# Feed-forwards of both streams: the next chunk's first inner tile ahead of a chunk's products down

## The reference

```python
def swiglu(h, w_in, w_out):
    a, b = jnp.split(h @ w_in, 2, axis=-1)
    return (jax.nn.silu(a) * b) @ w_out      # w_in 1024 x 5632, w_out 2816 x 1024

def _mlp(h, w1, w2):
    return jnp.square(jax.nn.relu(h @ w1)) @ w2   # w1 1024 x 4096, w2 4096 x 1024
```

## Time and profile before

| | |
|---|---|
| median of 3 runs | 3189.69 us (3185.83 to 3190.51) |
| the profiled execution's own time | 3183.49 us |
| its span | 3181.7 us |
| PE busy | 2898.7 us, 91% of the span |
| DVE, ACT, POOL busy | 1940.5, 1177.5, 549.0 us |
| granted TensorE clock, mean | 0.945 of full speed |
| HBM read | 408.60 MB, 129 GB/s over the span |

### The profile page before, as it was taken

The page is one execution under the profiler, slowest core; times in us unless marked ns, Lnnn a source line. Parts: engine busy times, 40 slices in busy tenths (PEclk is TensorE's granted clock), DMA queues, the critical chain, the costliest instruction groups (busy, mean ns, idle before and its releaser), DMA issues.

```text
span 3181.7 us, 38322 instructions
## 1 busy us (share of the span) xinstructions
PE 2898.7 (91%) x15190; PEld 2369.1 (74%) x15190; DVE 1940.5 (61%) x3141; ACT 1177.5 (37%) x1953; POOL 549.0 (17%) x561
## 2 busy tenths in 40 slices
PE   3899999988899998999998799899799998988797
PEld 2788887545788887888787799764777787845797
DVE  7888855645777857878555765542456664434554
ACT  3222234343422234222355554334432223335552
POOL 0000010322100010000101110113421113035431
PEclk7999999978999999999999899999899999989898
DMA  6556522101455534555322255220144432332453
GB/s 244 192 193 209 184 75 93 47 27 40 144 194 199 204 113 165 198 202 189 104 100 67 81 189 186 97 66 15 52 149 162 149 137 74 108 75 44 130 182 107
DMA packets 125283, 412.16 MB, mean 130 GB/s; under 512 B 25088, under 2 KB 27136, under 8 KB 124464
## 3 DMA queue, kind: packets, MB, share of 16 engines
q1 hardware_dynamic: 109552, 353.07, 33.1%
q0 software_dynamic: 15552, 56.63, 5.1%
HBM read 408.60 MB, written 1.05 MB: 129 GB/s over the span
## 4 chain that ended last, share of the span: by engine, by line
PE 80%; DVE 8%; ACT 7%; issue 2%; POOL 2%; DMA 1%; POOLq 0%; SPq 0%; ACTq 0%; DVEq 0%
PE bank L2132 24%; PE bank L2134 24%; PE bank L2133 24%; PE bank L2327 2%; POOL sb_temp L1124 1%; DVE sb_split_low L1664 1%; ACT sb_split_high L1266 1%; DVE sb_temp L1678 1%; PE bank L2288 1%; PE bank L2472 1%; DVE sb_rstd L1720 1%; DVE sb_temp L1728 1%; DVE sb_h_low L1734 1%; PE bank L2471 1%; PE bank L2317 1%
## 5 line engine op out<-in xcount | busy, mean ns | idle before, releaser
L2132 PE MATMUL bank<-sb_h_high,sb_split_high 128*128 128x256 f32 (+1 forms) x3048 | 1063.5, 349 | 107.2 <-DVE sb_h_low L1734 48.0
L2133 PE MATMUL bank<-sb_h_low,sb_split_high 128*128 128x256 f32 (+1 forms) x3048 | 1041.6, 342 | 0.0
L2134 PE MATMUL bank<-sb_h_high,sb_split_low 128*128 128x256 f32 (+1 forms) x3048 | 1040.8, 341 | 0.0
L1664 DVE TENSOR_TENSOR sb_split_low<-sb_raw,sb_split_high 128x1024 fp32r<-128x1024 f32 x515 | 639.0, 1247 | 237.0 <-ACT sb_split_high L1266 233.4
L2132 PEld LDWEIGHTS bank<-sb_h_high,sb_split_high 128*128 128x128 f32 x3048 | 592.4, 194 | 195.9 <-issue 61.9
L1266 ACT ACTIVATE sb_split_high<-sb_raw 128x1024 fp32r<-128x1024 f32 x515 | 536.0, 1050 | 369.5 <-DMA sb_raw<-weights 369.3
L2133 PEld LDWEIGHTS bank<-sb_h_low,sb_split_high 128*128 128x128 f32 x3048 | 595.0, 195 | 67.1 <-issue 0.5
L2134 PEld LDWEIGHTS bank<-sb_h_high,sb_split_low 128*128 128x128 f32 x3048 | 593.4, 195 | 67.0
L1678 DVE CUSTOM_DVE_ANT_0 sb_temp<-sb_ada_ffn,sb_cond_ffn 128x1024 bf16<-128x1024 f32 x408 | 479.5, 1219 | 11.8 <-ACT sb_cond_ffn L1270 8.1
L1784 DVE SCALAR_TENSOR_TENSOR sb_x_res<-bank,sb_gates,sb_x_res 128x256 f32<-128x256 f32 x296 | 133.1, 478 | 282.2 <-PE bank L2134 281.8
L2132 PE MATMUL bank<-sb_hidden_high_ffn,sb_split_high 128*128 128x512 f32 (+1 forms) x788 | 272.7, 346 | 0.0
(11 more groups left out here) (260 smaller groups left out, 3211.6 us busy)
## 6 DMA issues: line engine op xcount, KB each, us to landing
sb_raw<-weights SPq DMA_DIRECT2D x515, 512.0 KB, 3.3
sb_ada_ffn<-ada SPq DMA_DIRECT2D x114, 512.0 KB, 4.3
sb_ada_ffn<-ada POOLq DMA_DIRECT2D x90, 512.0 KB, 3.5
sb_ada_mlp<-ada SPq DMA_DIRECT2D x18, 512.0 KB, 4.2
sb_ada_mlp<-ada POOLq DMA_DIRECT2D x18, 512.0 KB, 4.3
sb_cond_ffn<-cond SPq DMA_DIRECT2D x3, 1024.0 KB, 5.3
sb_na_raw<-na_rpb SPq DMA_DIRECT2D x32, 96.0 KB, 5.8
sb_x_res<-tokens SPq DMA_DIRECT2D x1, 2048.0 KB, 15.4
```

The lines of the kernel that those rows point to most:

```text
L1664: do.tensor_tensor(m.low[i][:, :], m.raw[i][:, :], m.high[i][:, :].bitcast(F32), ALU.subtract).then_inc(*dve.mark("split_low", s))
L2132: do.matmul(out, ah, bh, start=start and j == 0, stop=False)
L2133: do.matmul(out, ah, bl, start=False, stop=False)
L2134: last = do.matmul(out, al, bh, start=False, stop=stop and j == len(terms) - 1)
```

## The change

While a chunk's products down are due, the first inner tile of the next chunk is worked out ahead of them: its up pieces come before the down pieces. `AHEAD = 1` is the number of such tiles, `ups_at` gives the first tile whose up pieces belong to a chunk, and the weight stream is laid out in the new order. One more hidden tile is held (`n_hidden`: nine buffers instead of eight in the stages of several chunks), and tile h lies in buffer h modulo that number, so that ACT's wait is for the chunk of the tile that lay there before. Stages of one chunk stay as they are.

```diff
--- before.py
+++ after.py
@@ -147,11 +147,12 @@
 
 def chunks(up, down, sizes):
 
-    n_up, out, at = len(up) // len(down), [], 0
+    n_up, out, at, done = len(up) // len(down), [], 0, 0
     for n in sizes:
         blocks = down[at:at + n].reshape(n, P, DT, P).transpose(2, 0, 1, 3).reshape(n, 8, P, P)
-        out += [up[at * n_up:(at + n) * n_up], blocks.transpose(0, 2, 1, 3).reshape(n, P, SLAB)]
         at += n
+        out += [up[done * n_up:(at + AHEAD) * n_up], blocks.transpose(0, 2, 1, 3).reshape(n, P, SLAB)]
+        done = at + AHEAD
     return np.concatenate(out)
 
 
@@ -161,6 +162,8 @@
           ("mla_down", 7), ("mla_uq", 6), ("mla_ukv", 4), ("mla_out", 8), ("mlp0", 64),
           ("na_fm", 16), ("na_tm", 8), ("na_out", 8), ("mlp1", 64)]
 N_SLABS = sum(n for _, n in STREAM)
+
+AHEAD = 1
 
 SIZES = {"ffn00": (8, 7, 7), "ffn01": (8, 7, 7), "ffn10": (8, 7, 7), "ffn11": (22,), "mlp0": (8, 8, 8, 8), "mlp1": (32,)}
 
@@ -321,11 +324,8 @@
 
 def up_slab(f, h, ab):
 
-    s, at = SLAB0[f], 0
-    for n in SIZES[f]:
-        if h < at + n:
-            return s + (h - at) * n_up(f) + ab
-        s, at = s + n * n_up(f) + n, at + n
+    c = next(c for c in range(len(SIZES[f])) if h < ups_at(f, c + 1))
+    return SLAB0[f] + h * n_up(f) + ab + chunk_at(f, c)
 
 
 def chunk_at(f, c):
@@ -333,8 +333,18 @@
     return sum(SIZES[f][:c])
 
 
+def ups_at(f, c):
+
+    return min(chunk_at(f, c) + AHEAD, sum(SIZES[f])) if c else 0
+
+
 def down_slab(f, c, block):
-    return SLAB0[f] + chunk_at(f, c + 1) * n_up(f) + chunk_at(f, c) + block // 8
+    return SLAB0[f] + ups_at(f, c + 1) * n_up(f) + chunk_at(f, c) + block // 8
+
+
+def n_hidden(f):
+
+    return max(SIZES[f]) + (AHEAD if len(SIZES[f]) > 1 else 0)
 
 
 def last_up(f):
@@ -466,7 +476,7 @@
     first = [[piece for h in range(head // per) for piece in up_pieces(f, h, part, ring)] for part in (0, 1)]
     body = []
     for c, n in enumerate(sizes):
-        for h in range(chunk_at(f, c), chunk_at(f, c + 1)):
+        for h in range(ups_at(f, c), ups_at(f, c + 1)):
             if h >= head // per:
                 body += up_pieces(f, h, p, ring)
         last = c == len(sizes) - 1
@@ -939,7 +949,7 @@
             self.bv = self.sb("na_bv", (P, D), own=own)
 
     def feed_forward_memory(self, f, own):
-        n = max(SIZES[f])
+        n = n_hidden(f)
         width = T if FFN[f][3] == BOTH else NX_TOK
         if FFN[f][2]:
             self.ada[f] = [self.sb(f"ada{i}_{f}", (P, D), own=own) for i in range(ADA_SLOTS)]
@@ -985,8 +995,7 @@
 
 def chunk_of(f, h):
 
-    c = max(c for c in range(len(SIZES[f])) if chunk_at(f, c) <= h)
-    return c, h - chunk_at(f, c)
+    return max(c for c in range(len(SIZES[f])) if chunk_at(f, c) <= h)
 
 
 
@@ -1351,10 +1360,10 @@
         first_of(f, h, p, bank, ACT.Relu, "relu")
 
     def hidden(f, h, p):
-        c, i = chunk_of(f, h)
+        i, before = h % n_hidden(f), h - n_hidden(f)
         act.wait_ge("hidden_raw" if FFN[f][0] == "swiglu" else "relu_squared", (f, h, p))
-        if c:
-            act.wait_ge("gemm", ("down", f, c - 1))
+        if before >= 0:
+            act.wait_ge("gemm", ("down", f, chunk_of(f, before)))
         do.activation(m.hidden[f][i][:, m.hidden_cols(f, p)], m.temp[h % 2][:, COLS[p]], identity).then_inc(
             *act.mark("hidden_high", (f, h, p)))
 
@@ -1769,7 +1778,7 @@
         do.tensor_tensor(temp, temp, src, ALU.mult).then_inc(*dve.mark("hidden_raw", (f, h, p)))
 
     def hidden_low(f, h, p):
-        i, cols = chunk_of(f, h)[1], m.hidden_cols(f, p)
+        i, cols = h % n_hidden(f), m.hidden_cols(f, p)
         dve.wait_ge("hidden_high", (f, h, p))
         do.tensor_tensor(m.hidden_low[f][i][:, cols], m.temp[h % 2][:, COLS[p]], m.hidden[f][i][:, cols].bitcast(F32),
                          ALU.subtract).then_inc(*dve.mark("hidden_low", (f, h, p), (f, h)))
@@ -2187,11 +2196,12 @@
         free(bank)
         for t in range(n):
             b = k * n + t
-            s = down_slab(f, c, b)
+            s, h = down_slab(f, c, b), chunk_at(f, c) + t
+            i = h % n_hidden(f)
             pe.wait_ge("split_low", s)
-            pe.wait_ge("hidden_low", (f, chunk_at(f, c) + t))
+            pe.wait_ge("hidden_low", (f, h))
             last = products(m.bank[bank][:, 0:T if p == BOTH else NC_TOK], [
-                (None, *columns_of(s % SLOTS, b % 8), m.hidden[f][t][:, cols], m.hidden_low[f][t][:, cols])],
+                (None, *columns_of(s % SLOTS, b % 8), m.hidden[f][i][:, cols], m.hidden_low[f][i][:, cols])],
                 start=t == 0, stop=t == n - 1)
             keys = [("x", f, c, k, p), ("down", f, c)] if t == n - 1 else []
             if b % 8 == 7:
```

## The result

The changed kernel took 3162.93 us, the median of 6 runs (3159.36 to 3167.47), beside 3185.99 us for the kernel before in 6 runs (3178.44 to 3190.51). The ratio, taken over all the runs and not from the two medians, is 0.993, with a 95% interval of 0.9915 to 0.9945. As a difference that is 17.5 to 27 us: the runs alone leave my sum of 17.6 us just inside. I had forecast 3172 us with a range of 3165 to 3179.

What follows compares the result with a forecast made beforehand. PE, busy 91% of 3181.7 us, bounds the kernel; time comes only from its waits or lower clock. Waits of 12.7 plus clock of 4.9 make 17.6 us; 3189.7 less that gives 3172 us, range 3165 to 3179.

Steps and rivals of the forecast that it cites:

- item 1: mlp0's first three chunks: tile 7's up product gains 5.63 us, so all 12.7 us of PE waits go.
- item 4: Tile 8's square beside DVE's dots or low half costs 0.83 us once, leaving margins of 0.2, 0.2 and 0.8 us.
- rival A: mlp0's waits shrink to about 2.1 us and still cost the clock, 3174 to 3179 us; chance 0.09.
- the prediction's bracket: Seven tiles before tile 7 give PE 4.87 us: 7 times 3 matmuls, with 24 matmuls taking 5.63 us.
- item 2: In the three stretches behind mlp0's waits, PE's clock stays up and all 4.9 us lost come back.
- items 3: Tile 8's piece is earlier, not new work; POOL's loads of slabs 4 and 6 fall behind its square, costing nothing.
- item 5: Three swiglu streams, six boundaries: PE waits 0.0 us there, so nothing can be won and slack only grows.
- Rival C: Swiglu products down: DVE falls behind in its adds and PE waits for a bank, 3196 us; chance 0.05.
- Rival B: No change, 3190 us: slab load behind tile 8's square on POOL makes tile 7's chain some 5.6 us longer; chance 0.06.

Runs made afterwards that it cites:

- swiglu alone: The first tile worked ahead in ffn00, ffn01 and ffn10 only, not in mlp0, against the changed kernel's edit: 3187.53 us, ratio 1.0002 to the kernel before.
- load late: Changed kernel with POOL's loads of slabs 2, 14 and 26 of mlp0 moved behind the square of the tile ahead: 3184.90 us, ratio 0.9999 to before.
- two extra squares: Changed kernel with two extra POOL squares ahead of the slab load for tiles 7, 15 and 23, each waited for: 3184.30 us in one run.
- one and four extra squares: Changed kernel with one or four extra POOL squares ahead of the load for tiles 7, 15, 23: 3169.22 us (4 runs), 3180.99 us (one run).

## Why the prediction missed its range

**The waits (item 1): right.** 12.7 us, all three, and nowhere else. But 12.7 us is one execution's figure. In the profile of the kernel before, run again, tile 7's square at the first boundary took 1.43 instead of 2.11 us, and the three waits were shorter:

```profile
PE bank L2132 <- DVE sb_hidden_low_mlp L1774: 11.4, 3, 3.9
```

The spare time came out at 0.8, 0.9 and 0.8 us at the three boundaries, where item 4 had 0.2, 0.2 and 0.8. At the first the load went out 2.26 us after the up product (2.93 before), as the square took 1.44 us there, and that made up for the contention; it did not land earlier for going out alone (3.60 us against 3.49), as rival A's "against" had it. The 4.87 us for the seven tiles is what the starts in the trace give; by the quotient in the prediction's bracket it would be 4.93, and the changed kernel shows 4.89.

**The clock (item 2): right, a little small.** 18.1 us less 12.7 of waits is 5.4 us, against 4.9 in the sum. The half microsecond between them stays open.

**What the tile brings along, and the contention (items 3, 4): right.** The square beside the dot cost 0.83 us and was covered. Slabs 4 and 6 go out behind the square of tile 8 and hold nothing up.

**The swiglu stages (item 5): right.** No gain and no loss that the runs show, by the kernel with them alone, ratio 1.0002. Rival C never came near. **Rival B** was rightly told from the code: made real, it ended where the prediction put it.

**The step that failed is the last one, from the sum to a time.** "Against the median: 3189.7 - 17.6" took the median of three runs as the kernel's level. Another 23 runs of the same program gave 3184.9, so the level was about 4.8 us too high, and that is half of the 9.2 us between 3172.1 and the measured 3162.93. The other half, 4.4 us, lies in the six runs of the changed kernel, which came out below what a level of 3184.9 less 17.6 gives. And the low end, "the profiled execution's level less the sum with a microsecond of scatter", gave the executions one microsecond, where single runs of one program spread over 13 to 15 us and two medians of six runs of the changed kernel lie 4 us apart. The prediction itself had named 6.4 us as what a measurement can tell, and did not put it into the range. With the level of 23 runs the same sum gives 3167.3 us; the second measurement of the changed kernel was 3167.08, which would have been inside the range. So whether the forecast landed in its range hung on which runs were drawn, and that close agreement is partly luck too. The difference of 23.1 us in the first comparison is 17.8 in the second, and the stretch that the change touches has 17.0 to 18.1 us in the profiles. Scatter is thus enough for the excess, and no place was found for a real gain. What makes a run fall low or high is open, and so is whether the 4 us between the two measurements are scatter alone: the later comparisons ran on three different chips, where the kernel before had medians of 3184.9, 3186.7 and 3184.1, and the chip of the first one is not on record.

## What to carry to other kernels

Before a tile is worked ahead to hide a late one, ask what makes it late. Here it was one load in POOL's program, behind POOL's own square, and two dots ahead of the low half. Moving the load, or moving the dots behind the low half, gave the same time within the scatter, with no new order of the products and no spare buffer. A timed sum should be set on a level from many runs, and its range should hold the scatter between runs even where every term of the sum is certain; three runs don't show it.

## What the runs showed of the hardware that I had not expected

**In one pair of executions, over half of the difference outside mlp0 sits in a stage where PE idles often, and shows as granted clock.** The odd mixer (the mixer of the first block's second layer) is the same code in the kernel before and in the one with swiglu alone. These are its stretches in the two profiles, the columns as in the earlier trace rows:

```profile
1579.10:1943.50 364.40, 329.66 (x2316) 303.01 (x2317) 221.11 (x345) 190.30 (x322) 42.85 (x37) 0.93 0.35 116
```

```profile
1576.70:1937.80 361.10, 324.93 (x2317) 299.17 (x2317) 221.11 (x346) 190.24 (x322) 42.82 (x37) 0.95 0.35 117
```

It took 364.40 us at a clock of 0.93 and 361.10 at 0.95, with DVE, ACT and POOL equally busy; PE is idle for 35 and 36 us in it. The feed-forward ahead of it differs by 0.2 us. These 3.3 us are over half of the 6.2 us by which the rest of the span differs between the two (2894.8 and 2888.6). The Trainium skill, page "TensorE: Matmul & The Clock Gate", Part 1, says that the number of slow matmuls at the start of one and the same kernel changes from run to run. It says so of the start; the two stretches here show as much in the middle of one. Why some runs fall better than others I did not try.

**The clock's price hardly follows the length of a wait.** Waits of 0.17 and 0.29 us left the clock at 1.00 behind them. Of the 18 waits of 2.89 to 4.92 us in six profiles, 17 (3.57 us and more) have a mean of 0.68 to 0.81 in the 7.30 us behind them, which is 1.4 to 2.3 us lost, and the shortest, 2.89 us, has 0.59, or 3.0 us. Two waits of the same 4.44 us in different kernels cost 1.7 us (clock 0.77, the kernel before) and 2.3 us (0.68, load late). Over a whole stretch of mlp0, what is left when the 268.8 us and the waits are taken off is 5.4 to 6.0 us for three waits of 11.2 to 14.1 us together, and 7.5 us for the kernel with two extra squares (11.1 us). No wait on a hidden tile's low half lay between 0.3 and 2.9 us, so where the price begins is open.

**A POOL load's landing goes along with what SP issues around it.** From POOL's issue to the first dot it took 3.42 to 3.66 us when SP's last issue lay 2 us or more back and its next one followed after 1.8 us or more (the first boundary of the kernel before in two executions, of the changed one in two, of those with one and four extra squares). It took 4.24 us in the earlier trace rows and 4.58 us in the late-load kernel when SP had sent a weight slab and a modulation slab 1.3 to 1.8 us ahead, and 5.06 us when both followed within 0.72 us. No run changes SP's issues alone, so this is what goes together, not a shown cause.
